# Forget gates with their weights as the stationary operand, gate and up columns sharing units in a feed-forward stage's last step, and every engine's list in a new order

## What is computed

```python
def conv_ffn(h, w_up, conv_w, conv_b, w_down):          # block 1; D_FF = 2816
    u = causal_dwconv(h @ w_up, conv_w, conv_b)
    g, up = jnp.split(u, 2, axis=-1)
    return (jax.nn.silu(g) * up) @ w_down

def swiglu(x, w_gate, w_up, w_down):                    # block 2; D_FF_2 = 2816
    return (jax.nn.silu(x @ w_gate) * (x @ w_up)) @ w_down

h = rms_norm_2(x, mix_norm[l])                          # mixer of block 2
proj = h @ w_in[l] + b_in[l]
q, k, v, f_logit, xr, gr, g_attn, g_rnn = jnp.split(proj, SPLIT_POINTS, axis=-1)
log_f = jax.nn.log_sigmoid(f_logit.astype(jnp.float32)) # f_logit: 8 columns, one per head
c = jnp.cumsum(log_f, axis=1)                           # enters the attention logits
```

## Time and profile before

| | |
|---|---|
| time before, median of 3 runs | 1928.38 us (1926.94 to 1928.7) |
| the profiled execution's own time | 1928.72 us |
| its span, first to last instruction | 1926.9 us |
| PE busy | 98% of the span |
| VectorE, ScalarE, GpSimd busy | 62%, 57%, 2% |
| mean granted TensorE clock | 0.993 of 2.4 GHz |
| transfers | 340.86 MB, mean 177 GB/s |

### The profile page before, as it was taken

The page is one execution under the profiler, slowest core; times in us unless marked ns, Lnnn a source line. Parts: engine busy times, 40 slices in busy tenths (PEclk is TensorE's granted clock), DMA queues, the critical chain, the costliest instruction groups (busy, mean ns, idle before and its releaser), DMA issues.

```text
span 1926.9 us, 23554 instructions
## 1 busy us (share of the span) xinstructions
PE 1892.6 (98%) x9148; PEld 1575.3 (82%) x9148; DVE 1200.8 (62%) x1767; ACT 1094.6 (57%) x1590; POOL 39.7 (2%) x61
## 2 busy tenths in 40 slices
PE   7999999989999999999999999999999999999999
PEld 6878888878888888888878788888888887888888
DVE  6767768576777655457865554454454686664544
ACT  6766555775646534459864544454444796545442
POOL 2000000000000000000000100000000001000000
PEclk9999999999999999999999999999999999999999
DMA  6535445445554555544555555455553445544553
GB/s 220 186 131 197 154 174 197 153 150 167 186 208 156 183 197 192 175 144 167 179 204 175 175 198 195 168 188 207 178 185 122 174 163 198 187 166 172 204 191 108
DMA packets 157578, 340.86 MB, mean 177 GB/s; under 512 B 5990, under 2 KB 18891, under 8 KB 156955
## 3 DMA queue, kind: packets, MB, share of 16 engines
q1 hardware_dynamic: 154208, 327.24, 49.0%
q0 software_dynamic: 2800, 11.91, 2.0%
q10 hardware_dynamic: 459, 0.20, 0.0%
HBM read 338.24 MB, written 1.09 MB: 176 GB/s over the span
## 4 chain that ended last, share of the span: by engine, by line
PE 89%; DVE 5%; ACT 2%; DMA 2%; issue 1%; POOL 1%; DVEq 0%; ACTq 0%; POOLq 0%
PE bank L450 28%; PE bank L452 27%; PE bank L451 27%; DVE w_lo L2011 2%; PE bank L557 1%; PE bank L546 1%; PE bank L772 1%; DMA t<-by_key 1%; PE bank L1027 1%; ACT w_hi L1250 1%; DMA raw<-in_ffn_w_gate 1%; ACT tmp L1530 1%; PE bank L511 1%; DVE tmp L2347 0%; PE bank L816 0%
## 5 line engine op out<-in xcount | busy, mean ns | idle before, releaser
L2011 DVE TENSOR_TENSOR w_lo<-raw,w_hi 128x1024 fp32r<-128x1024 f32 x620 | 730.2, 1220 | 216.6 <-ACT w_hi L1250 210.3
L1250 ACT ACTIVATE w_hi<-raw 128x1024 fp32r<-128x1024 f32 x620 | 631.3, 1055 | 303.1 <-PE bank L452 172.7
L450 PE MATMUL bank<-w_hi,r_hi 128*128 128x512 f32 (+1 forms) x1792 | 691.2, 386 | 1.5 <-DVE r_lo L2035 1.4
L452 PE MATMUL bank<-w_hi,r_lo 128*128 128x512 f32 (+1 forms) x1792 | 680.6, 380 | 0.0
L451 PE MATMUL bank<-w_lo,r_hi 128*128 128x512 f32 (+1 forms) x1792 | 679.9, 379 | 0.0
L450 PEld LDWEIGHTS bank<-w_hi,r_hi 128*128 128x128 f32 x1792 | 339.1, 189 | 67.0 <-issue 2.5
L452 PEld LDWEIGHTS bank<-w_hi,r_lo 128*128 128x128 f32 x1792 | 338.7, 189 | 64.3
L451 PEld LDWEIGHTS bank<-w_lo,r_hi 128*128 128x128 f32 x1792 | 339.2, 189 | 60.1
L450 PE MATMUL bank<-w_hi,z_hi 128*128 128x512 f32 x656 | 259.0, 395 | 1.7 <-DVE w_lo L2011 1.7
L452 PE MATMUL bank<-w_hi,z_lo 128*128 128x512 f32 x656 | 256.0, 390 | 0.0
L451 PE MATMUL bank<-w_lo,z_hi 128*128 128x512 f32 x656 | 255.4, 389 | 0.0
(11 more groups left out here) (208 smaller groups left out, 1399.0 us busy)
## 6 DMA issues: line engine op xcount, KB each, us to landing
raw<-in_w_in SPq DMA_DIRECT2D x79, 1024.0 KB, 5.3
raw<-in_w_up SPq DMA_DIRECT2D x44, 1024.0 KB, 5.3
raw<-in_ffn_w_gate SPq DMA_DIRECT2D x44, 1024.0 KB, 5.2
raw<-in_ffn_w_up SPq DMA_DIRECT2D x44, 1024.0 KB, 5.7
raw<-in_ffn_w_down SPq DMA_DIRECT2D x44, 1024.0 KB, 5.3
raw<-in_w_down SPq DMA_DIRECT2D x22, 1024.0 KB, 5.0
raw<-in_w_out SPq DMA_DIRECT2D x16, 1024.0 KB, 5.0
raw<-in_w_o_rnn SPq DMA_DIRECT2D x8, 1024.0 KB, 5.0
```

Source lines behind the costliest of these rows:

```text
L450: pe.matmul(out_, lh, rh, start=start, stop=False, skip_group_check=True)
L452: return pe.matmul(out_, ll, rh, start=False, stop=stop, skip_group_check=True)
L1250: A_(w_hi[:, n % NH, :], raw[:, u % NS, HALF * h:HALF * (h + 1)], ACT.Copy).then_inc(hi_ready, 1)
L2011: return V.tensor_tensor(dst, src, hi.bitcast(F32), ALU.subtract)
```

## The change

Three things are changed together.

1. **Forget gates.** The weights `wf_hi`/`wf_lo` become the stationary operand (128 columns from the eight of this k on; the columns behind them give rows of the result that nobody reads), and all 256 positions of `r_hi`/`r_lo` move. The result stands with heads on partitions; ScalarE copies it (`forget_copy`), PE turns it back (`forget_turn`, two transposes), and VectorE goes on as before. Two small memsets on GpSimd pad the weights.
2. **Last step of a feed-forward stage.** A unit now holds four k of 256 gate and 256 up columns side by side (two transfers of 512 KB), and the step is four `quarter` parts of 12 matmuls with 512 columns, like the other steps.
3. **Lists in a new order** on PE, ScalarE and VectorE, throughout.

```diff
-    return (6 * j - 2, 6 * j, 6 * j + 2) if j < STEPS - 1 else (28, 29, 30)
+    return (6 * j - 2, 6 * j, 6 * j + 2) if j < STEPS - 1 else (28, 28, 30)
...
+            def pairs(u, gate, up, col, up_col, half):
+                s = u % NS
+                sp.wait_ge(lo_ready, 2 * (u + 1 - NS))
+                dst = raw[:, s, :].rearrange("p (k m) -> p k m", k=4)
+                for w, c, at in ((gate, col, 0), (up, up_col, 256)):
+                    wv = w.rearrange("(k p) m -> p k m", p=P)
+                    sp.dma_start(dst[:, :, at:at + 256], wv[:, 4 * half:4 * half + 4, c:c + 256]
+                                 ).then_inc(raw_full[s], 16)
...
-                        narrow(u0 + ug, gate, CW * j)
-                        narrow(u0 + uu, up, up_col + CW * j)
+                        for half in range(2):
+                            pairs(u0 + ug + half, gate, up, CW * j, up_col + CW * j, half)
...
                 def forget_logits():
                     pe.wait_ge(rh_ready, KT * norm_at(where, 1) + KT)
+                    pe.wait_ge(wf_padded, 2)
+                    for k in range(KT):
+                        c = (l * KT + k) * H2
+                        mm = three(bank[C][:, 0:256], wf_hi[:, c:c + P], wf_lo[:, c:c + P], r_hi[:, k, :], r_lo[:, k, :],
+                                   k == 0, k == KT - 1)
+                    mm.then_inc(f_done, 1)
+                def forget_turn():
+                    pe.wait_ge(f_staged, l + 1)
                     for t in range(TB):
-                        for k in range(KT):
-                            mm = three(bank[C][:, t * H2:(t + 1) * H2], r_hi[:, k, t * P:(t + 1) * P],
-                                       r_lo[:, k, t * P:(t + 1) * P], wf_hi[:, l, k, :], wf_lo[:, l, k, :],
-                                       k == 0 and t == 0, k == KT - 1)
-                    mm.then_inc(f_done, 1)
+                        mm = pe.transpose(bank[C + 1][:, t * H2:(t + 1) * H2], sums_f[:, t * P:(t + 1) * P],
+                                          ident[0:H2, 0:H2])
+                    mm.then_inc(f_turned, 1)
...
+                def forget_copy():
+                    act.wait_ge(f_done, l + 1)
+                    if l:
+                        act.wait_ge(st_by_key, 16 * l)
+                    A_(sums_f[:, 0:256], bank[C][0:H2, 0:256], ACT.Copy).then_inc(f_staged, 1)
```

Of the lists, these pieces of the PE list are spoken of below (attention of block 1, and the loop of `ffn_conv`):

```diff
                 turn(where, 2)
                 scores(where, 4)
+                part(5, 1)
                 turn(where, 3)
...
                 scores(where, 5)
                 weigh(where, 4)
+                scores(where, 6)
                 turn_diff(where)
-                scores(where, 6)
                 turn(where, 5)
...
                     up_part(j, 0)
+                    up_part(j, 1)
                     turn_conv(f, j, 0, 0)
-                    turn_conv(f, j, 0, 1)
-                    up_part(j, 1)
                     up_part(j, 2)
                     up_part(j, 3)
                     down_half(u0, f, j - 1, 0, 0)
                     down_half(u0, f, j - 1, 0, 1)
-                    down_half(u0, f, j - 1, 1, 0)
-                    down_half(u0, f, j - 1, 1, 1)
+                    turn_conv(f, j, 0, 1)
                     turn_conv(f, j, 1, 0)
                     turn_conv(f, j, 1, 1)
+                    down_half(u0, f, j - 1, 1, 0)
+                    down_half(u0, f, j - 1, 1, 1)
```

More of the change, by code:

```diff
@@ L44 @@
 UNITS = LAYERS * (U1 + U2)
+SHARED = {f0 + 28 + half for half in range(2) for f0 in
+          [U1 * n + U_WIN + U_WOUT for n in range(LAYERS)]
+          + [LAYERS * U1 + U2 * n + m for n in range(LAYERS) for m in (0, U_FFN + U_MIX)]}
 C1_ATTN, C1_FFN, C1_SUB, C1_QK, C1_CONV, C1 = 0, 8, 16, 17, 21, 197
@@ L240, in half0, with landed @@
             block, layer = where
-            return 23 * layer if block == 1 else 23 * LAYERS + 50 * layer
+            return 22 * layer if block == 1 else 22 * LAYERS + 48 * layer
+        def landed(u):
+            n = 0
+            for b in range(u % NS, u + 1, NS):
+                n += 2 if b in SHARED else 1
+            return 16 * n
         def norm_at(where, n):
@@ L378, in _ @@
             nc.gpsimd.memset(eps[:, :], EPS).then_inc(eps_set, 1)
+            for tile in (wf_hi, wf_lo):
+                nc.gpsimd.memset(tile[:, N_WF:].bitcast(F32), 0.0).then_inc(wf_padded, 1)
             pool.dma_start(onehot, a["const_onehot"]).then_inc(ld_rel, 16)
@@ L690, in ffn_conv @@
                 turn_x(where, n, 7)
+                gate_part(0, 1)
                 gate_part(0, 2)
@@ L956, in _ @@
                 part(2, 2)
+                scores(where, 0)
                 part(2, 3)
@@ L991, in _ @@
                 turn(where, 6)
+                weigh(where, 6)
                 out_part(0, 1)
-                weigh(where, 6)
+                turn(where, 7)
                 out_part(1, 0)
-                turn(where, 7)
                 weigh(where, 7)
@@ L1113, in out_part @@
                     quarter(u + 36 + n, n // 2, i, (C, E)[n % 2], z_hi, z_lo, None, m_tiles if n < 2 else None)
+                turn_x(where, 1, 4)
                 part(0, 0)
-                turn_x(where, 1, 4)
-                part(0, 1)
                 turn_x(where, 1, 5)
@@ L1121, in _ @@
                 turn_x(where, 1, 7)
+                part(0, 1)
                 part(0, 2)
@@ L1169, in _ @@
                 part(9, 0)
-                scores(where, 0)
                 part(9, 1)
@@ L1173, in _ @@
                 part(9, 3)
+                scores(where, 0)
+                gate_part(0, 0)
+                gate_part(0, 1)
                 turned(7)
                 scores(where, 1)
-                gate_part(0, 0)
-                gate_part(0, 1)
                 gate_part(0, 2)
                 gate_part(0, 3)
+                scores(where, 2)
                 gated_part(0, 0)
                 turn(where, 0)
-                scores(where, 2)
                 gated_part(0, 1)
@@ L1350, in ffn_plain @@
                     hi(uj, 1)
-                    silu(j, 0)
                     hi(uj + 1, 0)
@@ L1430, in ffn_conv @@
                 norm_hi(where, n, 7)
-                hi(u0 + 2, 1)
+                deviation_x(where, n)
                 hi(u0 + 3, 0)
@@ L1505, in ffn_conv @@
                 hi(u0 + 32, 0)
+                prod_hi(4, 1)
+                copy_gate(5, 0)
+                copy_gate(5, 1)
                 main(5, 0, 0)
-                prod_hi(4, 1)
+                main(5, 1, 0)
                 hi(u0 + 32, 1)
+                silu(5, 0)
+                prod_hi(5, 0)
                 hi(u0 + 33, 0)
-                silu(5, 0)
-                main(5, 1, 0)
-                prod_hi(5, 0)
                 hi(u0 + 33, 1)
```

717 lines of the change are left out of this document (346 added, 371 removed).

## The result

The changed kernel takes 1906.8 us (median of 4 runs, 1906.47 to 1907.25), against 1927.92 before in the same comparison; the ratio is 0.9891, 95% interval 0.9874 to 0.9908. The forecast was 1907. That it was met so closely is partly luck: several terms of the sum were wrong, in opposite directions, so the rows come first.

What follows compares the result with a forecast made beforehand. PE bounds the kernel, busy 1892.6 of 1926.9 us. Terms -3.8 (units), -13.0 and +0.4 (forget gates), -7.9 (lists), +2.5 (new waits) sum to -21.8 on 1928.7: 1907 us, range 1898 to 1917.

Steps and rivals of the forecast that it cites:

- forget gates, with their turning: Mixer, both layers: 24 matmuls of 256 columns replace 48 of 8, later 512s at full clock, -13.0; added transposes +0.4.
- shared units: Last step of six feed-forward stages: 96 matmuls of 256 columns become 48 of 512, 0.63 us less each, -3.8.
- lists, attention of block 1: PE's waits at `turn(3)` and `turn_diff`, both layers, covered by work moved ahead: -1.7 us each.
- lists, mixer: PE's waits in the mixer for `nmax` (-2.7 us) and `w_lo` (-1.7 us) go, both layers.
- new waits in `ffn_conv` and mixer: Closer order: twelve places, half missed by 0.4 us, +2.5, between 0 and 12 x 1.0.
- the four terms of the lists: Waits of PE at `turn(3)`, `turn_diff`, `nmax` and the mixer's `w_lo`: -1.7, -1.7, -2.7, -1.7, given as -7.9 us.
- the first rival: Lists on all engines: waits reappear a part later, list gain 0 to 4, time 1911 to 1917 us; chance 0.22.
- `turn_diff` and `turn(3)`: Attention: `scores(6)` fills 0.86 us of `turn_diff`'s wait, `part(5, 1)` covers `turn(3)`'s division wait; -1.7 us each over both layers.
- The walk: Step of `ffn_conv`: from the end of `down_half`, low half ready at 6.4 us, wanted at 6.7, margin 0.3 us.
- The rival with more gain: Two low-clock places cleared, 4.7 us, and no new waits, 2.5 more: 1900 to 1902, to 1897 us; chance 0.11.
- the stall at 1091.8 us: Clock at 0.79 until 1099.5, PE idle 2.1 us and about 1.2 lost to the clock; no edit named touches it.
- The two falls of the clock: Around `turn_diff` of layer 0 (0.50, 103 to 106 us, 1.4 spared) and 1091.8 to 1099.5 us (0.79).

Runs made afterwards that it cites:

- experiment 1: The kernel before with the new forget gates alone, their result read four halves later: 1914.76 us, ratio 0.9933.
- experiment 2: The kernel before with the shared gate and up units alone and the last step's lists that belong to them: 1922.66 us, ratio 0.9975.
- 9: The kernel before with new forget gates and shared units, old order of lists except the last step's and the forget gates' calls: 1912.94 us, ratio 0.9924.
- experiment 5: The changed kernel with the old forget gates, 48 matmuls of 8 columns in one run, without the copy and two transposes: 1921.3 us.
- 10: The changed kernel with the old order of all three engines in the attention of block 1, both layers: 1908.66 us.
- 11: The changed kernel once more, nothing changed, measured beside the kernel with the old attention order: 1907.28 us.
- experiment 7: The changed kernel with product(j, 0) put ahead of two low halves on VectorE in the loop of `ffn_conv`: 1909.45 us.
- experiment 6: The changed kernel with the old forget gates in four pieces of 12 narrow matmuls, a part between any two, without copy and transposes: 1913.95 us.
- experiment 3: The kernel before with the new lists of all engines alone, old forget gates and old last-step units: 1925.08 us, ratio 0.9982.
- 4: The changed kernel with scores(6) moved back behind turn_diff on PE: 1905.95 us.
- 8: The changed kernel with pair 5 started earlier at the end of block 1's attention, scores(5) ahead of part(5, 3): 1907.13 us.

## Why the prediction was right, and where it was not

| term | predicted | shown |
|---|---|---|
| forget gates, with their turning | -12.6 | -13.5 (experiment 1); -9.7 (2 to 9), -14.5 (5) |
| shared units | -3.8 | -3.5 in their stages (2); -1.8 (1 to 9) |
| lists, attention of block 1 | -3.4 | -0.6 (10, 11: twice layer 1) |
| lists, mixer | -4.4 | -3.8 (9), -2.2 (against 1) |
| lists, head of `ffn_plain` | 0 | -1.1 by the wait, up to -1.4 more by the clock (9) |
| new waits in `ffn_conv` and mixer | +2.5 | 0 (trace, 7) |
| sum | -21.8 | -21.9 between the profiled executions, -21.1 between the medians |

The column of what was shown comes from different pairs of kernels and need not add up to the last row. What is clear is that 2.8 too much was put on the attention of block 1, that 2.5 was charged for waits that did not come, and that the head of `ffn_plain` was left out. The total came out right because these cancel, which the prediction had no reason to expect. Two slips of arithmetic did not matter: the four terms of the lists sum to 7.8 and not 7.9, and the bounds of the first rival ("1911 to 1917") are not those of the sums beside them, which give 1915 to 1916.

*Forget gates.* Right in mechanism, and in size as far as the pairs of kernels agree. The reason for the size, that half of the gain is the clock and belongs to the long run of narrow matmuls, is shown by experiments 5 and 6, not only by its absence afterwards. The Trainium skill ("TensorE: Matmul & The Clock Gate", Back-to-back issue gap) puts an isolated matmul's distance at columns over the clock plus about 2.5 ns, and at some 25 ns for 64 columns or fewer; it adds that in a stream with weight loads this counts too little for small operands. By it one of 256 columns would stand 0.109 us from the next and one of 8 columns 0.025. Here they stand 0.117 and 0.104 apart, so the trace is near the rule for 256 columns and at four times the page's figure for 8, in the direction that the page's remark on weight loads gives, and the measurement decides.

*Shared units.* Right, 0.6 us a stage in the traces of experiment 2. Not foreseen was that they also relax what the next step asks for (experiment 3: 2.4 us).

*`turn_diff` and `turn(3)`.* This step failed: "What was idle is filled with 0.86 of work that had to be done anyway". `scores(6)` had been filling the next idle stretch, ahead of `turn(5)`. Four orders of this attention (before, changed, 4, 8) wait 7.4 to 8.9 us in all, whoever is named as the releaser; the waits of both layers are added, with those put down to the issue. What holds it is the chain of pair 5 through the other two engines. ScalarE in the changed kernel:

```profile
96.76 1.28 ACT L1531 ACT_TABLE_LOAD   x1
98.05 0.30 ACT L1531 ACTIVATE gstd<-gss,eps 128x8 f32<-128x8 f32 x1
98.26 0.85 ACT L1553 ACTIVATE tmp<-bank 128x384 f32<-128x384 f32 x2
99.13 1.28 ACT L1540 ACT_TABLE_LOAD   x1
100.42 0.51 ACT L1540 ACTIVATE tmp<-tmp,nmax 128x256 f32<-128x256 f32 x1
```

It is busy without a gap from there until 103.7, with 2.56 us of it for two loads of tables. That this chain is the cause is argued from these rows and from the three orders that did not help; a kernel with fewer loads was not run. The rival "The lists give nothing back" described this stretch rightly, and this stretch alone. For `turn(3)` the named wait did go, and what the attention of layer 1 gained by both moves together is 0.3.

*New waits.* The walk was right to 0.1 us and the conclusion drawn from it was not. A margin of 0.3 us was treated as a risk with a price of 2.5; but durations repeat so closely in these traces that it was met in every step, and when it was taken away (experiment 7) the wait was 0.27 in all six.

*The rival with more gain* said of the stall at 1091.8 us that no edit touches it. The diff has the edit, `gate_part(0, 0)` ahead of `turn_x(where, n, 4)` in `ffn_plain`, and it is worth 1.1, or 2.5 where the clock would have fallen. The two falls of the clock that this rival counted on belong to no order alone: neither is in every execution.

## What to carry to other kernels

Before a piece of work is moved into an idle stretch, look at what it covers where it stands: if the next call waits for the same chain, only the name of the wait changes, and the sum of the waits over the whole stretch is the number to compare. A margin walked from a profile of such fixed lists was met in all six places or missed in all six, so it is not priced by a chance of its own for each. A missed one costs more than the wait that is listed: 0.54 for 0.27 here, since the wait is counted from the end of a matmul that the next would have overlapped. Slow matmuls behind a wait are to be looked up in a second trace before they are put down to an order. And a narrow operand costs twice: by its own start-to-start time and by the clock that a long run of it takes from the wide work behind.

## What the runs showed of the hardware

A matmul of 8 columns stands 0.104 us from the next at full clock, about as much as 235 columns at the rate of the 512s (0.2268). A load of its 128 x 128 stationary operand stands with each of them, 0.11 apart too; whether that sets the pace was not tested. In all eight runs of 48 that were profiled (four kernels, two layers) the clock fell to 0.50 of full speed while PE was busy throughout, and 7 to 13 matmuls of 512 columns behind the run were slow, a number that differs between the profiled executions; in the eight pieces of 12 of one execution, with 12 wide matmuls between, it did not fall. Behind waits of 0.9 to 2.1 us it fell in some executions and not in others: one execution of the changed kernel fell to 0.57 for eight matmuls, 1.5 us, and the other did not, and the same holds for the places at 103 us and at the head of `ffn_plain` (experiments 9 and 10). The spread of the kernel before is 6.2 us over 21 executions, that of experiment 5 8.1 over six. Of the seven kernels without narrow matmuls, four or five executions at a time lay within 2.7 us, but for one execution (1911.63, beside three from 1905.72 to 1908.37). That the long runs alone make the spread is not shown: the pieces of experiment 6 spread over 4.8 us in four executions.
